# A layer step with window-cache copies moved from the SyncE queue to the ScalarE queue

## The reference

```python
h = rmsnorm(x, norm_g)
proj = h @ w_in                       # (2048, 1024) x (1024, 4104)
qkv = silu(causal_conv4(proj[:, :1536]))            # new_conv = last 3 raw rows of 1536 channels
o_a = gated_delta_rule(q, k, v, g, beta, s0) ...    # 4 heads, chunks of 64, exact
o_b = dilated windows (128,1), (512,4), (2048,16)   # 8 heads of 64
y = x + concat(o_a * silu(z_a), o_b * silu(z_b)) @ w_out;  y = rmsnorm(y, final_norm_g)
# for the decoding sequences the window caches move on by 4 rows:
new_k = concat([k_win, kb], axis=1)[:, -2048:]      # (8, 2048, 8, 64), the same for v
```

## Time and profile before

| | us |
|---|---|
| median of 3 runs (2035.49 to 2042.34) | 2039.32 |
| the profiled execution's own time | 2042.34 |
| its span in the trace | 2040.6 |
| PE busy in the span | 1782.3 (87%) |
| ACT busy | 595.8 (29%) |
| DMA engines' mean share of the span, the queue q1 | 56.8% |

### The profile page before, as it was taken

How to read it: one execution, slowest core, us unless ns; L and a number is a source line. 1 busy time by engine, 2 the same in 40 slices (tenths; PEclk the granted TensorE clock), 3 DMA queues, 4 the chain that set the end, 5 groups by cost and what they waited for, 6 DMA issues and landing times. The chain is left out here.

```text
span 2040.6 us, 27583 instructions
## 1 busy us (share of the span) xinstructions
PE 1782.3 (87%) x9730; PEld 1425.1 (70%) x9730; DVE 747.0 (37%) x1757; ACT 595.8 (29%) x1483; POOL 316.6 (16%) x351
## 2 busy tenths in 40 slices
PE   1999999999999998808588899889997559999997
PEld 1997888888888886707487788778875426556663
DVE  3424412521531350155644444444442422322321
ACT  3423312411321230111324344344344302222211
POOL 0000000000000000025032432332243411121210
PEclk6999999999999999959798898899888559999998
DMA  6423576676458679799337546634441574655550
GB/s 135 116 69 123 167 232 184 169 192 203 162 177 211 183 157 129 214 223 289 107 73 176 136 98 150 162 108 105 114 114 28 173 183 142 179 155 172 159 165 26
DMA packets 250185, 309.18 MB, mean 152 GB/s; under 512 B 70269, under 2 KB 198781, under 8 KB 240589
## 3 DMA queue, kind: packets, MB, share of 16 engines
q1 hardware_dynamic: 250068, 307.64, 56.8%
HBM read 228.01 MB, written 146.44 MB: 184 GB/s over the span
## 5 line engine op out<-in xcount | busy, mean ns | idle before, releaser
L322 PE MATMUL pj<-hT_hi,w_hi 128*128 128x512 f32 x896 | 360.1, 402 | 1.8 <-DVE raw L549 1.8
L324 PE MATMUL pj<-hT_hi,w_lo 128*128 128x512 f32 x896 | 352.6, 394 | 0.0
L323 PE MATMUL pj<-hT_lo,w_hi 128*128 128x512 f32 x896 | 352.3, 393 | 0.0
L324 PEld LDWEIGHTS pj<-hT_hi,w_lo 128*128 128x128 f32 x896 | 168.7, 188 | 38.4
L322 PEld LDWEIGHTS pj<-hT_hi,w_hi 128*128 128x128 f32 x896 | 169.0, 189 | 37.0 <-issue 2.1
L323 PEld LDWEIGHTS pj<-hT_lo,w_hi 128*128 128x128 f32 x896 | 169.1, 189 | 34.7
L1449 PE MATMUL o_ps<-pt,vt 128*65 128x256 f32 (+3 forms) x560 | 151.6, 398 | 4.3 <-DVE ot L1671 2.2
L656 POOL IOTA row_at<- 128x1 int32 x1 | 0.1, 138 | 865.1 <-POOLq L2429 865.1
L1513 ACT ACTIVATE pt<-pt_ps 128x512 f32<-128x512 f32 x144 | 84.8, 589 | 157.8 <-PE pt_ps L1427 157.4
L2193 PE MATMUL y_bank<-wo_hi,mh 128*128 128x512 f32 (+1 forms) x272 | 112.2, 412 | 7.4 <-POOL ml L2178 5.3
L517 DVE SCALAR_TENSOR_TENSOR acc<-raw,conv_wt,acc 128x512 f32<-128x512 f32 x144 | 108.2, 752 | 5.1
(11 more groups left out here) (441 smaller groups left out, 3369.0 us busy)
## 6 DMA issues: line engine op xcount, KB each, us to landing
out_dram<-in_cache_k_win_dram SPq DMA_DIRECT2D x56, 584.0 KB, 7.1
out_dram<-in_cache_v_win_dram SPq DMA_DIRECT2D x56, 584.0 KB, 7.1
w_raw<-in_w_in_dram SPq DMA_DIRECT2D x32, 512.0 KB, 10.8
qk_ch<-sil SPq DMA_DIRECT2D x32, 256.0 KB, 3.1
z_ch<-xr SPq DMA_DIRECT2D x32, 256.0 KB, 3.7
wqk<-hi SPq DMA_DIRECT2D x32, 256.0 KB, 5.2
wqk<-lo SPq DMA_DIRECT2D x32, 256.0 KB, 5.2
sc_class<-qk_ch SPq DMA_DIRECT2D x32, 256.0 KB, 4.4
```

What stands on the lines that cost most here:

```text
L322: pe.matmul(out, w_hi[s][:, k, :], hT_hi[:, k, cols], start=(k == 0), stop=False)
L323: pe.matmul(out, w_hi[s][:, k, :], hT_lo[:, k, cols], start=False, stop=False)
L324: mm = pe.matmul(out, w_lo[s][:, k, :], hT_hi[:, k, cols], start=False, stop=(k == KT - 1))
```

## The change

The 112 copies leave SP's order in `project` and are issued by ACT in `mixers` instead: in each head h, right behind the copy of `pt` of units 0 to 6 one piece of sequence h's key cache, behind those of units 7 to 13 one piece of its value cache. The sizes are the same. The semaphore `shifted` becomes one of the phase, and ACT waits for all of it at the end of `mixers`; SP's wait at the end of `sample` is gone. The three stores of `conv_tail` move from behind the tile za of the last column group to behind the last tile of all, right ahead of SP's final waits in `project`.

```diff
@@ constants @@
-    env.shifted = nc.alloc_semaphore(name="shifted")
@@ project, block.sync @@
-            def shift(i):
-                b, piece = divmod(i, 2 * PIECES)
-                old, new = (D.cache_k, D.out_k) if piece < PIECES else (D.cache_v, D.out_v)
-                at = PIECE * (piece % PIECES)
-                sp.dma_start(new[b, at:at + PIECE, :], old[b, at + DEC_SEQ:at + DEC_SEQ + PIECE, :]).then_inc(env.shifted, 16)
...
                 for c in range(NCH):
                     cs = slice(CHUNK * c, CHUNK * (c + 1))
-                    shift(NCH * t + c)
...
-                if j == NJ - 1 and kind == "za":
-                    sp.wait_ge(tail_done, 3 * NJ)
-                    with nc.allow_non_contiguous_dma(reason="the last three rows of a channel-major tile"):
-                        for r in range(TAIL):
-                            sp.dma_start(D.new_conv[r].rearrange("(t p) -> p t", p=P), conv_tail[:, :, r]).then_inc(tail_stored, 16)
+
+            sp.wait_ge(tail_done, 3 * NJ)
+            with nc.allow_non_contiguous_dma(reason="the last three rows of a channel-major tile"):
+                for r in range(TAIL):
+                    sp.dma_start(D.new_conv[r].rearrange("(t p) -> p t", p=P), conv_tail[:, :, r]).then_inc(tail_stored, 16)

             sp.wait_ge(tail_stored, 16 * TAIL)
@@ mixers @@
+        shifted = sem("shifted")
@@ mixers, block.scalar @@
+            def shift(b, old, new, piece):
+                rows = slice(PIECE * piece, PIECE * piece + PIECE)
+                after = slice(PIECE * piece + DEC_SEQ, PIECE * piece + PIECE + DEC_SEQ)
+                act.dma_start(new[bass.ds(b, 1), rows, :], old[bass.ds(b, 1), after, :]).then_inc(shifted, 16)
...
                     act.activation(pt[:, k % CUTS, 0:w], pt_ps[k % 2][:, 0:w], ACT.Copy).then_inc(S["turned_out"], 1)
+                    if k < PIECES:
+                        shift(h, D.cache_k, D.out_k, k)
+                    elif k < 2 * PIECES:
+                        shift(h, D.cache_v, D.out_v, k - PIECES)
...
             walk(act, attend, delta)
+            act.wait_ge(shifted, 16 * 2 * PIECES * DEC_BATCH)
@@ sample, block.sync @@
-            sp.wait_ge(E.shifted, 16 * 2 * PIECES * DEC_BATCH)
```

## The result

| | before | after |
|---|---|---|
| median us (lowest to highest, runs) | 2039.03 (2035.49 to 2042.34, 4) | 2058.19 (2054.79 to 2064.89, 4) |
| the profiled execution's own time | 2042.34 | 2059.47 |
| its span | 2040.6 | 2057.7 |

After to before is 1.0099, with a 95% interval of 1.0078 to 1.0119: the change makes the kernel slower by about 1%. The forecast was 2051 us, slower, with a range of 2039 to 2069. Between the two profiled executions lie 17.1 us of span; they are what follows accounts for.

A forecast was written before the change was run, and what follows sets the result against it. PE was taken to bound the kernel nearly everywhere. The terms -12.3 + 17.6 + 1 + 2 + 3 = +11.3 us gave 2053.6 on the profiled execution and 2051 for the median, with a range of 2039 to 2069.

The forecast's parts named there:

- ACT's issues: Mixers: 14 copy issues a head on ACT mostly fit its idle time; +1 us heads 1 to 6, +2 last head.
- The stall goes: Projection near 806 us: PE's 9.31 us wait and 3.0 us from half clock disappear; -12.3 us.
- The tail at the end: Projection's end: SP and barrier wait 21 us for conv_tail stores, delaying the next phase; +17.6 us.
- Copies leaving SP: Projection: 112 issues and 67 MB leave, but PE had no gap to fill; 0.
- The DMA share: Mixers' heads: copies add 0.42 to 0.54, giving 0.96 of the DMA engines, close to full but not over.
- The inverse in head 0: Head 0: copies delay the inverse that SP stores and loads again; +3 us, ends 0 and 8.
- backlog: Head 0: of nine copies issued, about one and a half, 3 us, stand before the inverse's store and load.
- rival C: Mixers don't hide the copies: +24 us over the heads, head 0 8; +37, 2077 us; chance 0.13.
- The end of the mixers: Mixers' end: ACT's wait for all copies costs 0, with some 18 us of cover.
- SP's wait in `sample`: End of sample: the wait goes, but the copies were long done; 0.
- B: Rival: tail lands in 5.1 us on an idle queue, ACT's slack hides all copies; -10.6, 2029 us; chance 0.10.
- D: Rival, the middle way: tail 13 us, +9.6, and mixers at 3; +0.3, no change, 2040 us; chance 0.17.

The follow-up runs named there:

- e1: Kernel after with the three conv_tail stores back in their old place, copies still on ACT; 2046.24 us, 1.0034 to before.
- e2: Kernel before with only the conv_tail stores moved to the end of the phase, copies still on SP; 2053.34 us, 1.0055 to before.
- e9: Kernel after with head 0's copies issued two at a time in units 10 to 16; 2052.33 us, 1.0061 to before.
- e10: Kernel after with head 0's copies in units 0 to 7 and 10 to 15, none in 8 and 9; 2055.03 us, 1.0071 to before.
- e5: Kernel after with head 0's copies issued two in each of units 9 to 15, none in 0 to 8; 2059.71 us, 1.008 to before.
- e4: Kernel after with each copy cut from 292 rows to 16, other rows not copied, same issues on ACT; 2053.49 us, 1.0052 to before.
- e8: Kernel after with tail stores on SP ahead of head 7, head 0's copies two in each of units 9 to 15; 2034.64 us, 0.9954 to before.
- e6: Kernel after with each copy halved and two issued behind each pt, 28 a head, same bytes; 2070.51 us, 1.0114 to before.
- e7: Kernel before with the three tail stores moved into the mixers on SP ahead of head 7, copies staying in the projection; 2032.5 us, 0.9937 to before.
- e3: Kernel after with the tail stored by one contiguous-row transfer of the same 18 KB, values in another order; 2035.32 us, 0.9975 to before.

## Why the prediction was right, step by step

It was right in direction and in its range, and low in size: it said +11.3 us on the profiled execution, where 17.1 were measured, and 2051 for the median, which came out at 2058. In its own terms: 11.3 - 0.4 (stall) + 6.4 (tail) + 1.9 (inverse) - 2.6 (ACT's issues) + 1.8 (rest of head 0) - 1.2 (the -1.4 and +0.2 of the account) = 17.2. That ACT's term was too high hid a part of the tail's miss; that is luck.

- *The stall goes, -12.3.* Measured -12.7 at the last matmul. Right, with its mechanism: e1 brings the stall back with the stores alone. Nothing else was late, as said.
- *The tail at the end, +17.6.* Measured +24.0, the larger miss: 27.6 us from the first tail issue to the next phase where 21 were taken. The start was right (862.9 less 12.3 is 850.6, and it was 850.24). The size was not. I had the upper reading, 24.0, from the earlier trace rows and took 3 us off it, because a copy and a weight load had stood around it. In after nothing stood there and the last store still landed in 24.6 us, from an issue 1.4 us behind the first, 26.0 in all; SP and the barrier took 1.6 more. So of the 6.6 us between 21 and 27.6, 3.0 are the discount, 2.0 the longer landing and 1.6 what follows it. e2, with the copies still in the queue, gives 27.5. The discount was wrong: the traffic around the stores had next to no part in it. Its upper end of 25 us, +21.6, was passed too.
- *The rule of the Trainium skill* (Perfetto Trace Analysis, "DMA Instruction — HWDGE"), that the last descriptor waits for the written data: the trace after agrees more plainly than the earlier trace rows did, in the window 865 to 876 us, where no transfer is on record and all still wait.
- *Copies leaving SP, 0.* Measured by e1 as -2.6 us with the tail in its old place and by after against e2 as -0.65 (848.81, 849.46), which is inside the 2.2 us by which equal projections differ. Right for this change, since the tail was moved too.
- *ACT's issues, +1 in heads 1 to 6 and +2 in the last.* Measured +0.4 (head 1 to head 7) and 0.0. An issue takes 0.52 us, as taken from SP's row, and nothing on PE waits longer for ACT because of it: PE's products with `pt` wait 4.2 us in all, against the 4.3 of the earlier trace rows:

```profile
L1442 PE MATMUL o_ps<-pt,vt 128*65 128x256 f32 (+3 forms) x560 | 151.9, 399 | 4.2 <-issue 2.1
```

- *The DMA share, 0.96 in a head.* It came out at 0.83: the copies added 0.29 where 0.42 had been worked out from the projection's 279 GB/s. It harmed no steady head either way.
- *The inverse in head 0, +3.* Measured +4.9, within its ends of 0 and 8, for a reason that was only partly right. The step that failed is the backlog. It counted nine copies up to "unit 8" (the last copy of `pt` in the earlier trace rows, at 1008.15, is the tenth and unit 9's) and had a pile of one and a half of them stand before the store and the load. Only the stores' leg is slower; the loads' leg is not. By e9, e10 and e5 the earlier eight make about 1 us and the last two about 4. The place, the wait and who suffers were right. The rule of the Trainium skill (DMA: Bandwidth & Descriptors, "Queues, rings and completion order"), that each engine takes turns among the queues packet by packet, is not contradicted by what was seen: the wait depends on what is in flight then, and hardly on how much was queued before. I had read it as a few packets, and so nearer 3 than 8; but a copy's packets are of 18.7 KB. That the size of the packets decides was not tested by itself; e4, which changed bytes and sizes together, only excludes the issues.
- *Left out:* the rest of head 0, +1.8, which is PE at a granted clock of 0.88 for 0.92, with no more waiting. The prediction said of rival C that a gap on PE can be followed by a stretch at the lower clock, but priced none behind the inverse. What decides between the two clocks stays open. The same stretch in e8 and e9:

```profile
1010.50:1071.63 61.13, 53.19 (x352) 47.13 (x352) 30.85 (x103) 13.74 (x42) 21.57 (x22) 0.92 0.73 211
1032.32:1094.72 62.40, 54.49 (x352) 48.38 (x352) 30.82 (x103) 13.71 (x41) 21.53 (x22) 0.88 0.77 227
```

e8 moves copies all through it, behind 17.73 us of PE's idle, and has the 0.92; e9, behind 13.83 us, has the 0.88. So neither the bytes nor the length of the idle alone decides it.

- *The end of the mixers, 0, and SP's wait in `sample`, 0.* Right: +0.0 at the first issue of `sample`.

The rivals: B needed a landing in under 9.7 us; it was 27.6 with the wait. C, 3 us a head, fell with the account, and in e6 even twice the issues don't make a steady head longer. D would have needed the tail at 13.

## What to carry to other kernels

A transfer of single elements to DRAM is priced by who waits behind it, not by its bytes: before moving one, list everything that queues or waits behind the new place, and make it contiguous or put it beside long work whose queue has nothing urgent (0.55% lost at a phase's end, 0.63% won in a busy head, each against the kernel before). When bulk copies are moved under work that seems to have room for them, look for the few short transfers in that stretch that an engine waits for, and leave out the two or three copies right ahead of them; the mean DMA share tells nothing of those. For a size, take the row as it stands; a discount for its surroundings needs a row of its own. And before a step of 2 or 3 us in an account is given a cause, look at the busy time and the granted clock of that stretch, and at the same stretch in other kernels.

## What the runs showed of the hardware

- Three stores of 1536 elements of 4 bytes each, from SBUF to DRAM, land 11 to 25 us after their issue in and behind the projection, whether the queue is full or empty (13.7/19.7/22.7 before, 11.3/22.0/24.6 after). In after the transfer records end at least 11 us before the completion. In e8, with copies on another queue beside them, they took 19.5/25.5/44.8; for e7 no landing is on record.
- Behind them, where others followed at once (before and e1), the queue took one more transfer and then hung: 22.19 us on a copy, 23.05 us on a store. So the kind of transfer that hangs doesn't matter.
- The same 18 KB in one transfer with contiguous rows: 3.7 us from its issue to the next phase's first (e3), against 27.6 in after.
- A DMA issue costs ACT what it costs SP, 0.52 us, but can take longer where two follow each other: the first of a pair 2.38 us in e5, a pair 2.75 us in e6.
- Two copies of 584 KB on ACT's queue, issued 2.7 and 0.2 us ahead of a 512 KB store on SP's, lengthen SP's wait behind that store from 2.9 to 7.3 us (e5). Eight copies, the last 5 us ahead of it, lengthen it to 4.0 (e10).
- The same 352 matmuls keep PE busy for 52.9 to 53.4 us at a granted clock of 0.92 and for 54.5 to 55.4 at 0.88, in twelve traces of one stretch of head 0.
